# A decoder step on one core: attention heads in pairs, memory heads spread behind projection tiles, first expert loads into other places

## What is computed

```python
gb, u, q, k, v = split_projection(x, w_in)            # conv gates and input, q, k, v of 12 heads of 64
conv_out = gb * short_conv(u, w_conv)
attn_out = dilated_attention(q, k, v, rel_bias_table) # the sample: over cache_win_k, cache_win_v
x = layer_norm(ALPHA * x + concat([conv_out, attn_out]) @ w_out)
q = x @ w_mem_q                                       # 4 heads of 256 over 256 memory tokens
probs = softmax(q @ mem_k.T / 16)                     # prompt: mem_k = mem_prompt @ w_mem_k, mem_v alike
x = layer_norm(ALPHA * x + (probs @ mem_v) @ w_mem_o) # the sample: over cache_mem_k, cache_mem_v
idx, gates = top4(softmax(x @ w_router + b_router))   # 4 of 32 experts
for e in range(32):                                   # gate_up 1024 x 2048, down 1024 x 1024
    g, u = split(x[e] @ w_gate_up[e] + b_gate_up[e])
    y += gates * (((u + 1) * g * sigmoid(1.702 * g)) @ w_down[e] + b_down[e])
x = layer_norm(ALPHA * x + y)
```

## Time and profile before

| | us |
|---|---|
| median of 3 runs | 1305.15 |
| lowest, highest | 1305.01, 1306.88 |
| the profiled execution | 1304.69 |
| its span, first to last instruction | 1302.9 |

### The profile page before, as it was taken

The page is one execution under the profiler, slowest core; times in us unless marked ns, Lnnn a source line. Parts: engine busy times, 40 slices in busy tenths (PEclk is TensorE's granted clock), DMA queues, the critical chain, the costliest instruction groups (busy, mean ns, idle before and its releaser), DMA issues.

```text
span 1302.9 us, 16399 instructions
## 1 busy us (share of the span) xinstructions
PE 1228.6 (94%) x6566; PEld 576.0 (44%) x6566; DVE 375.4 (29%) x921; ACT 202.1 (16%) x334; POOL 39.0 (3%) x62
## 2 busy tenths in 40 slices
PE   9999999989999999999989898989989898999996
PEld 7994457675634343343323333333323333332332
DVE  4646533561532213122130212202130212212123
ACT  4442311131211010110101011010101011010001
POOL 2201000100000000000000000000000000000001
PEclk9999999999999999999999999999999999999999
DMA  9984876587959999999999999999999999999993
GB/s 326 266 288 163 252 249 259 194 319 296 394 197 416 429 426 426 427 429 427 429 428 427 427 428 427 429 427 428 427 427 429 428 427 428 428 427 428 427 426 161
DMA packets 62628, 485.08 MB, mean 372 GB/s; under 512 B 6176, under 2 KB 6516, under 8 KB 34336
## 3 DMA queue, kind: packets, MB, share of 16 engines
q1 hardware_dynamic: 58720, 469.46, 88.3%
q0 software_dynamic: 3872, 15.12, 3.6%
HBM read 479.40 MB, written 5.17 MB: 372 GB/s over the span
## 4 chain that ended last, share of the span: by engine, by line
PE 62%; DMA 31%; DVE 3%; ACT 1%; SPq 1%; issue 1%; POOL 0%; DVEq 0%; ACTq 0%; POOLq 0%
PE ps L2022 28%; DMA ring<-in_w_gate_up_dram 16%; DMA late<-in_w_gate_up_dram 13%; PE ps L1620 10%; PE ps L2080 6%; PE ps L2062 5%; PE ps L1653 4%; DMA ring<-in_cache_mem_v_dram 1%; PE ps L1994 1%; PE ps L1790 1%; DMA arena<-in_b_gate_up_dram 1%; PE ps L2088 1%; PE ps L1808 1%; PE ps L1600 1%; DVE arena L1228 1%
## 5 line engine op out<-in xcount | busy, mean ns | idle before, releaser
L2022 PE MATMUL ps<-ring,arena 128*64 128x512 f32 x1536 | 360.0, 600 | 15.1 <-DMA ring<-in_w_gate_up_dram 15.1
L1517 DVE TENSOR_TENSOR arena<-arena,ps 128x264 f32<-128x264 f32 x128 | 55.2, 431 | 573.4 <-PE ps L2080 573.4
L2022 PEld LDWEIGHTS ps<-ring,arena 128*64 128x64 f32 x1536 | 98.9, 136 | 200.4 <-issue 160.6
L2062 PE MATMUL ps<-ring,arena 128*64 128x512 f32 x768 | 171.3, 596 | 12.4 <-DMA ring<-in_w_down_dram 12.4
L2062 PEld LDWEIGHTS ps<-ring,arena 128*64 128x64 f32 x768 | 53.7, 137 | 116.3 <-issue 104.3
L958 ACT ACTIVATE arena<-arena 128x512 f32<-128x512 f32 x32 | 20.2, 632 | 470.6 <-DVE arena L1500 470.6
L2080 PE MATMUL ps<-arena 128*128 128x264 f32 x256 | 91.3, 438 | 0.0
L2022 PE MATMUL ps<-late,arena 128*64 128x512 f32 x384 | 90.0, 596 | 0.0
L1620 PE MATMUL ps<-arena,ring 128*128 128x256 f32 x384 | 87.2, 381 | 1.4 <-ACT arena L897 0.7
L2080 PEld LDWEIGHTS ps<-arena 128*128 128x128 f32 x256 | 38.1, 188 | 103.9 <-issue 103.9
L1620 PEld LDWEIGHTS ps<-arena,ring 128*128 128x128 f32 x384 | 71.0, 189 | 14.5 <-issue 3.3
(11 more groups left out here) (303 smaller groups left out, 992.3 us busy)
## 6 DMA issues: line engine op xcount, KB each, us to landing
ring<-in_w_gate_up_dram SPq DMA_DIRECT2D x96, 2048.0 KB, 34.0
ring<-in_w_down_dram SPq DMA_DIRECT2D x48, 2048.0 KB, 34.4
late<-in_w_gate_up_dram SPq DMA_DIRECT2D x16, 2048.0 KB, 33.8
arena<-in_w_gate_up_dram SPq DMA_DIRECT2D x16, 1024.0 KB, 32.2
late<-in_w_gate_up_dram SPq DMA_DIRECT2D x16, 1024.0 KB, 34.2
late<-in_w_down_dram SPq DMA_DIRECT2D x8, 2048.0 KB, 35.3
ring<-in_w_in_dram SPq DMA_DIRECT2D x12, 1024.0 KB, 14.9
ring<-in_cache_mem_k_dram SPq DMA_DIRECT2D x8, 1024.0 KB, 5.9
```

The source lines that it names most:

```text
L1517: nc.vector.tensor_tensor(xT[:, c, :], xT[:, c, :], ps[:, 2 + c % 2, 0:T], ALU.add).then_inc(e_y_out, 1)
L2022: ins = mm(ps[64 * j:64 * j + 64, 6 * a + gu, :], x, w[:, D * gu + 512 * j:D * gu + 512 * j + 512], start=(c < 0), stop=(c == 7), skip_gro ...
L2062: ins = mm(ps[64 * j:64 * j + 64, 4 + half, :], x, w[:, kk, 512 * half:512 * half + 512], start=(m == 0), stop=(m == 7), skip_group_check= ...
```

## The change

**Heads.** `scores` and `values` take a pair of heads, and their products alternate between the two. A round of the loop is now a pair: scores of pair d, transposes of head 2d-2, one or two fills (`FILLS`), with the transposes of head 2d-1 behind the first tile of a single fill or at the end of the first of two, then the values of pair d-1. ACT copies a pair's result at once. On DVE the key work of the round's first fill stands between the maxima of the even and the odd head, that of a second fill behind both normalisings. The transposes of the last head and the last pair's values move behind tiles 0 and 1 of `wout` half 0.

**Norms.** The wait for the last transposed columns moves from `layer_norm` behind the second tile of `wmq` half 0, and for the router into its chain of products, column by column. `sum_sample_queries` comes ahead of `wmq`.

**Memory heads.** They are spread behind tiles of `wmq` halves 2 and 3 and `wmo` half 0; the sample's path begins one half later and ends with `sample_squares` behind the last tile of `wmo`. On DVE the eight `key_scores` stand in seven places among the heads, and the last residual is ahead of the sample's variance and scaling. In the stream the first two halves of `wmo` come ahead of `mv` 0 to 3.

**Places.** `PLACES` gives unit 0 the two slots outside the ring, units 1 to 4 ring places 2, 4, 8, 10 (the `mv` slots), unit 5 the two separate slots, units 6 and 7 ring places 0 and 6 (the `wmo` slots).

```diff
+    s += [("wmo", i) for i in range(2)] + [("mv", b) for b in range(4)]
+    s += [("wmo", i) for i in range(2, 4)] + [("mv", b) for b in range(4, NS)]
...
+FILLS = ((0,), (1,), (2, 3), (4,), (5, 6), (7,))
...
+PLACES = (None, 2, 4, 8, 10, None, 0, 6)
...
+            for u in range(1, UNITS):
+                at = PLACES[u]
+                if at is None:
+                    sp.wait_ge(s_sat, 4)
+                else:
+                    reader_done(sp, NPRE + at - RING)
+                    reader_done(sp, NPRE + at + 1 - RING)
+                unit_load(0, u)
...
+                head_max(2 * d)
+                if d >= 1:
+                    key_work(fills[0])
+                head_max(2 * d + 1)
+                if d == 0:
+                    own_scores()
+                for h in (2 * d, 2 * d + 1):
+                    head_norm(h, ((0, 128), (128, 384)))
+                for b in fills[1:] if d else fills:
+                    key_work(b)
...
             sample_softmax(1, MH)
+            residual(48, 2, 4)
             sample_turned(1, MH)
-            residual(48, 0, 4)
             sample_pick(1)
+            residual(48, 4, 5)
             sample_parts(1)
+            residual(48, 5, 6)
             sample_sum(1)
-            residual(48, 4, 5)
+            residual(48, 6, 7)
             sample_centred(1)
-            residual(48, 5, 7)
+            residual(48, 7, 8)
             sample_variance(1)
             sample_scaled(1)
-            residual(48, 7, 8)
...
+            def scores(pair):
+                if pair >= 1:
+                    pe.wait_ge(s_nm, 2 * pair)
+                q, k = ([proj[E * i:E * i + E, x + pair, :] for i in both] for x in (Q0, K0))
+                for i in both:
+                    mm(ps[:, 4 + i, 0:P], q[i][:, 0:P], k[i][:, 0:P], start=True, stop=True)
+                for i in both:
+                    mm(ps[:, 4 + i, P:3 * P], q[i][:, P:2 * P], k[i][:, 0:2 * P], start=True, stop=True).then_inc(
+                        s_sc, 1)
...
+            dense_half("wmq", 0, queries, {1: rest_turned})
+            dense_half("wmq", 1, queries)
+            dense_half("wmq", 2, queries, {0: lambda: mem_scores(0), 1: lambda: mem_scores(1)})
+            dense_half("wmq", 3, queries, {0: lambda: mem_turned(0), 1: lambda: mem_values(0),
+                                           2: lambda: mem_turned(1), 3: lambda: mem_values(1)})
+            mem_scores(2)
+            mem_scores(3)
...
+            dense_half("wmo", 0, out_columns, {0: lambda: mem_turned(2), 1: values_then_turned,
+                                               2: lambda: mem_values(3)})
...
+            dense_half("wmo", 1, out_columns, {1: lambda: scores_turned(1, MH), 3: lambda: sample_probs(1, MH)})
+            dense_half("wmo", 2, out_columns, {0: lambda: sample_values(1, MH, "mv", D),
+                                               2: lambda: sample_values_turned(1, D)})
+            dense_half("wmo", 3, out_columns, {0: lambda: sample_dense(1, "wmo"), 1: lambda: sample_columns(1),
+                                               2: lambda: sample_means(1), 3: lambda: sample_squares(1)})
```

More of the change, by code:

```diff
@@ L58 @@
 KEYS_IN_TURN = (4, 5, 0, 1, 6, 7, 2, 3)
-KEYS_FIRST = 6
 SROWS = NP_ + NS - 32
@@ L128, in stream @@
         s += [("mqb", i), ("mk", 2 * i), ("mk", 2 * i + 1)]
-    s += [("mv", b) for b in range(4)] + [("wmo", i) for i in range(4)] + [("mv", b) for b in range(4, NS)]
+    s += [("wmo", i) for i in range(2)] + [("mv", b) for b in range(4)]
+    s += [("wmo", i) for i in range(2, 4)] + [("mv", b) for b in range(4, NS)]
     return s
@@ L496, in reader_done @@
                 piece_used(eng, 2 * i + 1)
-            elif what in ("wout", "wmo") and i < 2:
-                eng.wait_ge(s_sd, 1 if what == "wout" else 2)
+            elif what == "wout" and i < 2:
+                eng.wait_ge(s_sd, 1)
+            elif what == "wmo" and i < 3:
+                eng.wait_ge(s_sd, 2)
             elif what in GROUP0:
@@ L619, in unit_load @@
                         "a (p s v) n -> p (a s) (v n)", s=2, v=2)
-                w, done = u % UNITS, unit_landed(u)
-                if w == 1:
+                w, done, first = u % UNITS, unit_landed(u), unit_first(u)
+                if w and first is None:
                     for s in range(2):
@@ L1725, in _, with memory_half @@
             pe.wait_ge(s_nat_out, 4)
             pe.wait_ge(s_nat_act, 3)
-            for step in range(H + 1):
-                if step < H:
-                    scores(step)
-                if 1 <= step <= H:
-                    probs_turned(step - 1)
-                if step >= 2:
-                    values(step - 2)
-                f = FILL.get(step)
-                if f is not None:
-                    dense_half("wmv" if f < 4 else "wmk", f % 4, token_rows(memT))
+            def memory_half(f, behind=None):
+                dense_half("wmv" if f < 4 else "wmk", f % 4, token_rows(memT), behind)
@@ L1738, in memory_keys @@
+            for d in range(H // 2):
+                fills = FILLS[d]
+                second = (lambda: probs_turned(2 * d - 1)) if d else None
+                scores(d)
+                if d:
+                    probs_turned(2 * d - 2)
+                memory_half(fills[0], {len(fills) - 1: second} if d else None)
+                if len(fills) == 2:
+                    memory_half(fills[1])
+                if d:
+                    values(d - 1)
+            probs_turned(H - 2)
             def memory_keys(pair):
@@ new lines, in mem_turned, with mem_values @@
+            def mem_turned(j):
+                h = H + j
+                pe.wait_ge(s_pn, 2 * h + 2)
+                pe.wait_ge(s_pt_out, h)
+                for qc in range(2):
+                    for mc in range(2):
+                        ins = tp(ps[:, 6, MT * mc + P * qc:MT * mc + P * qc + P],
+                                 lg[:, h % 2, MT * qc + P * mc:MT * qc + P * mc + P], ident)
+                ins.then_inc(s_pt, 1)
+            def mem_values(j):
+                h = H + j
+                pe.wait_ge(s_pt_out, h + 1)
+                pe.wait_ge(s_av_out, h)
+                for ec in range(2):
+                    c0 = MT * j + P * ec
+                    for mc in range(2):
+                        ins = mm(ps[:, 7, NP_ * ec:NP_ * ec + NP_], memv[:, mc, c0:c0 + P],
+                                 pt[:, h % 2, MT * mc:MT * mc + MT], start=(mc == 0), stop=(mc == 1))
+                ins.then_inc(s_av, 1)
```

246 lines of the change are left out of this document (123 added, 123 removed).

## The result

| | before | after |
|---|---|---|
| median of the runs, us | 1306.01 (4 runs, 1305.01 to 1306.88) | 1288.45 (4 runs, 1286.44 to 1289.30) |
| profiled execution, us | 1304.69 | 1288.53 |
| its span, us | 1302.9 | 1286.7 |
| ratio, 95% interval | | 0.9869 [0.9857, 0.9880] |

The changed kernel is faster by 1.31%. Its profiled span is 16.2 us shorter where the prediction booked 11.7. The medians are 17.6 us apart here; in the rounds of the experiments the kernel before had medians of 1304.62 to 1305.61, so some 1.4 us of that is this round's 1306.01.

A forecast was written before the change was run, and what follows sets the result against it. The prediction took the expert weight stream as the bound, timed by PE's first expert. Gains of 10.1 + 1.2 + 0.4 = 11.7 us off 1304.69, plus 0.46 to the median, gave 1293.5 us, range 1286 to 1301.5.

The forecast's parts named there:

- What bounds it: Expert weight stream at a fixed rate: time moves one for one with PE's start of the first expert.
- Cover for the eight places: Expert buffer's eight places filled before PE's first expert, with over 10 us in hand.
- Part 1: Twelve heads in pairs: transpose waits gone, 2.5 us, and paired products cheaper, 7.6 us; 10.1 us in all.
- The page weighed: Skill page on pairs' matmuls: weight loads overlap only across row groups, so scores would gain and values not.
- rival C: Heads in pairs: only the values do not overlap, 3.0 us missing, 1296.5 us; chance 0.10.
- Rival B: Heads in pairs: halves do not run at once for short matmuls, 7.6 us missing, 1301.1 us; chance 0.10.
- Part 2 and 3: First norm and memory heads: gaps gone, 7.0 us, less 5.8 for the later last key block; gain 1.2 us.
- Part 4: Later sample path: router wait gone, 0.7 us, less 0.3 charged at the last residual; gain 0.4 us.
- Part 5: New order of the expert buffer's places: nothing late, worth 0 us.
- Rival E: Expert stream: new place order lowers its rate, each 1% costing 8.6 us, 1311 us at 2%; chance 0.08.
- Rival D: Heads in pairs: DVE holds PE if its 6.0 us grow beyond 9, about 1305 us; chance 0.05.
- Rival A: Memory heads: `mem_v` is not late, so the gaps give their 7.0 us, 1287.7 us; chance 0.15.

The follow-up runs named there:

- e7: Changed kernel with six extra 512-column matmuls on PE just before the first expert; 1293.00 us, ratio 0.9900.
- e5: Changed kernel with SyncE issuing the first `wmo` and `mem_v` loads ahead of the last key blocks, same slots and readers; 1279.96 us, ratio 0.9808.
- e1: Kernel before with the heads in pairs alone, everything else as before; 1290.04 us, ratio 0.9890.
- e10: Changed kernel with four 512-wide matmuls of a fill moved between the two heads' scores and between their values; 1298.53 us, ratio 0.9950.
- e2: Kernel before with everything of the change except the heads in pairs; 1301.94 us, ratio 0.9979.
- e6: Changed kernel with the first places in plain ring order; 1286.96 us, ratio 0.9859.
- e9: Changed kernel with both the earlier issue of `wmo` and `mem_v` loads and the places in plain ring order; 1279.96 us, ratio 0.9812.
- e3: Changed kernel with all products of a pair's even head before those of the odd one, in scores and values; 1289.31 us, ratio 0.9886.
- e4: Changed kernel with the even head's products before the odd head's in values alone, scores still alternating; 1289.29 us, ratio 0.9883.
- e8: Changed kernel with five throwaway 512-column matmuls filling PE's second wait, inside `sample_values`; 1288.69 us, ratio 0.9868.
- e11: Changed kernel with throwaway matmuls filling both PE waits, three ahead of the first `wmo` half and five inside `sample_values`; 1288.72 us, ratio 0.9870.

## Why the prediction was right, and where it was too small

**What bounds it: right.** The time moved with the first expert: 15.6 us there, 16.2 in the span and 17.6 in the medians; e7 and e5 confirm it from both sides, and so does the constant stretch of 929.1 to 930.3 us behind the refill. Cover for the eight places was booked at over 10 us and is 13.

**Part 1: right mechanism, term too small, 10.1 booked and 14.6 measured** (by e1's medians and by the stage). The step that failed is the price of a pair's products, 1.27 us. I took the gain of the scores by the row of a load of 128-wide weights, 0.77, and of the values 0.5, halfway between 0.2 and 0.75. Measured are 0.84 and 0.80, that is the whole of one head's products in both cases: 6 x 1.64 = 9.8 us instead of 7.6. The weights' loading, which I used as a floor, is no floor for two halves, since it runs beside itself as well: the trace has the twelve loads of a pair's values in 0.70 us, where the six of one head took 0.69 before. The waits at the transposes were 2.5 and went, as booked. The rest, 2.3 us, stood in no term: returning to the full shape. The twelve groups of transposes take 4.86 us, 0.41 each, before about 0.49 each: 1.0 us less. The steps of the eight fills and the first half of the output projection add up to 62.1 instead of 63.4 us. That is 2.3 together. e10, which has more such returns, is slower by just their price. The rows for it were in the trace of before, 6.87 beside 7.06 us for the same sixteen matmuls.

**The page weighed, rival C: wrong for this kernel.** The values' two heads differ in columns alone and run at once, 0.80 us for both. The Trainium skill, "TensorE: Matmul & The Clock Gate", section "Part 3: Packing small matmuls", has weight loads overlap matmuls only across row groups; here the trace does not agree. The same section of the Trainium skill also lists three column tiles at 2.38 times the speed, so the rival took one of its sentences by itself. Rival B falls with C: e10 shows what it costs when the halves do not run at once, 9.1 us.

**Part 2 and 3: right, 1.2 booked, 0.7 measured in the profile.** The gaps went, the last key block went out late, and PE waited for `mem_v` in the second half of `sample_values`, where I had put it. The last key block goes out 9.0 us earlier than before, and the second half of the output projection begins 14.1 us earlier, so the block is 5.1 later in its surroundings (booked 5.8). The loss at `mem_v` grew from 3.2 to 7.0 us. I had it grow from 1.5 to some 5, by about as much, but had read only the last wait of the earlier trace rows and so put the loss before too low. Of the 7.0, 1.4 is the lower clock (5.04 for 3.62), which I had not seen. The wait for `wmo`, which I named as possible and free, was 2.6 us and is free, since the second wait ends with a landing. Where the clock falls in the first wait and not in the second, this part is worth 1.4 us more. e2 has 2.7 us for parts 2 to 5 by the medians, where I booked 1.6 and the profile above has 1.4; that most executions have their fall in the first wait would explain it, but is not shown.

**Part 4: 0.4 booked, 0.7 measured.** The router's wait went (gain 0.7 as booked); the 0.3 that I charged for the sample path does not show, as the wait at the second norm is 0.40 us and was 0.52.

**Part 5: right,** by e6 and e9. Rival E with it: the rate is 428 GB/s over 1100 to 1200 us. Rival D: DVE never held PE in the pairs and had 16.5 us in hand.

**Rival A has the right number for the wrong reason.** It said 1287.7 with `mem_v` in time. The time came out 0.8 above that, but `mem_v` was late; the 4.5 us came from part 1. e5 is rival A made true, and it is 8.5 us faster still: 9.6 us in the profile, where A had 5.8 for it, since A knew neither the wait for `wmo` (2.6) nor the whole of the loss at `mem_v`. A total near a rival's figure says nothing for it as long as its row is not looked at.

## What to carry to other kernels

Two matmuls that use different halves of the array's rows or columns are worth pairing even when each is short: price the pair at one of them, and count each return from half shapes to the full one (0.15 to 0.19 us here) as well. Before work is spread ahead of a reader that frees a buffer, look at what is queued behind the load that waits for it; an in-order queue turns the delay of one block into a delay of all that follow, and issuing the others first gained more (8.5 us) than the spreading itself (2.7 with all the rest). A gain ahead of a saturated stream comes back one for one. That must end where the first buffers are no longer full in time; no run here came to that point, e6 was the nearest with some 4 us in hand.

## What the runs showed of the hardware that I had not expected

**Halves run at once whatever the order in the code.** Scores of two heads in turn take 0.87 us, alternating 0.86, one head 0.85. The Trainium skill, "TensorE: Matmul & The Clock Gate", section "Part 3: Packing small matmuls", states that matmuls start and end strictly in the order of the program. The records of e3 do not follow the order of the code, with the four of L1755 ahead of those of L1756. Whether TensorE got them in the order of the code no run shows, so this does not settle what the Trainium skill states there.

**A wait of 2.6 us can cost the clock, and where it falls decides who pays.** The changed kernel, e2, e3, e4, e6, e7 and e10 have both waits, and in the profiled execution of each the granted clock fell exactly once: behind the first wait, to 0.83 over 264 to 274 us, in e3, e6 and e7 (and in e8), or behind the second in the others, as in the changed kernel (0.83 over 290 to 300 us; by single microseconds 0.50 from 297 to 300). In e2 it stayed down for longer, 0.66 over 310 to 320 us, and took 2.9 us. PE had run without a gap before. It had stood idle for 2.5 to 2.8 us in the first case and twice for 1.5 us in the second. At a mean of 0.83 part of the stretch is at the lower of its two levels, 1.2 instead of 2.4 GHz. The same eight matmuls in e6, behind the first wait:

```profile
267.37 3.42 PE L1671 MATMUL ps<-arena,ring 128*128 128x256 f32 x8 [2.84 <-issue]
...
294.34 1.04 PE L1852 MATMUL ps<-ring,late 128*32 128x512 f32 x2 [0.34 <-DMA ring<-in_cache_mem_v_dram]
296.90 3.62 PE L1852 MATMUL ps<-ring,late 128*32 128x512 f32 x26 [1.51 <-DMA ring<-in_cache_mem_v_dram]
```

They take 3.42 us instead of 1.97, and the 1.45 lost shorten the next wait from 1.51 to 0.34: nothing is lost in the end, since that wait ends with a landing. Behind the second wait nothing waits for a load any more, and the 1.4 us are on the path. Why it is one or the other in a given execution stays open. With no waits (e5, e9) or with both filled (e11) it did not fall.
